# Reciprocals of the softmax denominators in the first attention: spread over partitions by products with the identity, or by GpSimd's transfers through DRAM

## The reference

```python
sc = jnp.einsum('...qd,...kd->...qk', qb, kk) * SCALE + bias      # causal mask inside
m = jnp.max(sc, axis=-1, keepdims=True)
p = jnp.exp(sc - m)
den = jnp.sum(p, axis=-1, keepdims=True)
o = jnp.einsum('...qk,...kd->...qd', p, vv) / den
# the three branches of B are added, each times its gate per row and head
```

## Time and profile before

| | |
|---|---|
| median of 3 runs | 2310.55 us (2309.71 to 2312.58) |
| profiled execution | 2309.23 us, span 2307.4 us |
| TensorE matmul busy | 2054.1 us, 89% |
| weight loads busy | 1079.7 us, 47% |
| VectorE busy | 999.7 us, 43% |
| ScalarE busy | 616.5 us, 27% |
| GpSimd busy | 184.1 us, 8% |
| mean granted TensorE clock | 0.954 of 2.4 GHz |

### The profile page before, as it was taken

How to read it: one execution, slowest core, us unless ns; L and a number is a source line. 1 busy time by engine, 2 the same in 40 slices (tenths; PEclk the granted TensorE clock), 3 DMA queues, 4 the chain that set the end, 5 groups by cost and what they waited for, 6 DMA issues and landing times.

```text
span 2307.4 us, 26770 instructions
## 1 busy us (share of the span) xinstructions
PE 2054.1 (89%) x10158; PEld 1079.7 (47%) x10158; DVE 999.7 (43%) x1830; ACT 616.5 (27%) x1191; POOL 184.1 (8%) x222
## 2 busy tenths in 40 slices
PE   7999999999999998989978986999749588959994
PEld 4555764444444444565566443333244466433331
DVE  2003652577872013687354244223156655252223
ACT  2003551000000013322254033334241344123332
POOL 3000110111110000121000001000010000000001
PEclk9999999999999999999999997999979899979997
DMA  8333002577664203112010026777442000066884
GB/s 277 99 86 123 30 2 73 203 244 264 237 237 146 82 16 119 37 37 73 1 56 1 19 115 219 297 300 278 163 166 73 1 1 1 1 230 261 325 323 185
DMA packets 103868, 311.64 MB, mean 135 GB/s; under 512 B 8839, under 2 KB 42791, under 8 KB 85312
## 3 DMA queue, kind: packets, MB, share of 16 engines
q1 hardware_dynamic: 73360, 178.50, 22.1%
q0 software_dynamic: 22576, 103.09, 12.7%
q10 hardware_dynamic: 7808, 28.35, 3.1%
HBM read 280.47 MB, written 34.68 MB: 137 GB/s over the span
## 4 chain that ended last, share of the span: by engine, by line
PE 76%; DVE 9%; issue 7%; PEld 2%; DMA 2%; ACT 1%; DVEq 0%; PEldq 0%; POOL 0%; POOLq 0%; ACTq 0%; SPq 0%
PE ps L2554 13%; PE ps L2293 10%; PE ps L302 8%; PE ps L327 7%; PE ps L1577 6%; PE ps L729 5%; PE ps L2275 5%; PE ps L764 4%; PE ps L1434 3%; PE ps L747 2%; DVE T L857 2%; PE ps L1553 2%; PE ps L2261 2%; PEld ps L1285 1%; PE ps L1285 1%
## 5 line engine op out<-in xcount | busy, mean ns | idle before, releaser
L2554 PE MATMUL ps<-wide 128*128 128x512 f32 x704 | 306.0, 594 | 2.3 <-issue 1.3
L2293 PE MATMUL ps<-wide,Z 128*64 x576 | 259.7, 604 | 4.0 <-DVE Z L2387 4.0
L2294 PE MATMUL ps<-T,Z 128*64 128x512 f32 x576 | 259.7, 605 | 0.0
L2554 PEld LDWEIGHTS ps<-wide 128*128 128x128 f32 x704 | 132.4, 190 | 171.8 <-issue 170.6
L793 ACT ACTIVATE T<-T,nm 128x128 f32<-128x128 f32 (+5 forms) x208 | 139.8, 672 | 171.7 <-DVE nm L857 171.7
L747 PE MATMUL ps<-ident,T 128*128 128x128 f32 x752 | 115.1, 284 | 46.6 <-DVE T L365 27.7
L2293 PEld LDWEIGHTS ps<-wide,Z 128*64 128x64 f32 x576 | 77.1, 139 | 158.0 <-issue 158.0
L1577 PE MATMUL ps<-wide 128*128 128x512 f32 (+1 forms) x384 | 149.7, 547 | 0.6 <-issue 0.6
L2275 PE MATMUL ps<-wide,Z 128*64 x288 | 134.6, 611 | 4.4 <-ACT Z L2348 4.4
L2276 PE MATMUL ps<-Z 128*64 128x512 f32 x288 | 134.7, 611 | 0.0
L1056 DVE SCALAR_TENSOR_TENSOR Z<-Z,wide 128x2048 f32<-128x2048 f32 x56 | 131.6, 2350 | 2.8
(11 more groups left out here) (350 smaller groups left out, 2807.7 us busy)
## 6 DMA issues: line engine op xcount, KB each, us to landing
wide<-in_experts SPq DMA_DIRECT2D x96, 1024.0 KB, 7.5
Z<-in_mod_w POOLq DMA_DIRECT2D x32, 1024.0 KB, 5.3
moe_out<-Z ACTq DMA_DIRECT2D x36, 512.0 KB, 5.0
X<-in_mod_w POOLq DMA_DIRECT2D x16, 1024.0 KB, 5.2
wide<-in_w_gate SPq DMA_DIRECT2D x22, 512.0 KB, 5.0
wide<-in_w_up SPq DMA_DIRECT2D x22, 512.0 KB, 6.8
wide<-in_w_in SPq DMA_DIRECT2D x10, 1024.0 KB, 10.9
wide<-in_w_down SPq DMA_DIRECT2D x10, 1024.0 KB, 5.1
```

The lines of the kernel that those rows point to most:

```text
L2293: pe.matmul(ps[low, p, :], mo.xT[:, p, c, low], w.columns(e, j, at), start=(c == 0), stop=(c == DK - 1))
L2294: last = pe.matmul(ps[high, p, :], mo.xT[:, p, c, high], mo.wgu[:, p, j, at:at + 512], start=(c == 0), stop=(c == DK - 1))
L2554: last = pe.matmul(self.gu.bank(u)[:, 0:self.n], w, self.rhs(c), start=(c == 0), stop=(c == DK - 1))
```

## The change

The first attention gets an argument `far`: a DRAM scratch of 16 x 8 x 128 floats and four buffers of 128 x 512 in the part of `X` that holds nothing at that time. With it

- TensorE leaves out L774 and the wait for `recips_done`, and the ring of PSUM banks has no entry for it.
- GpSimd, for each pack, waits for `recips_done`, stores `rd` (128 partitions x 8 floats) to DRAM with queries along the row, which makes 1,024 pieces of one float; waits until that has landed; and loads it back with two transfers, one for each head, each row of 128 floats four times into 64 partitions (64 x 4 pieces of 512 B). Between the store and the loads it waits for the pack four before to be scaled, whose buffer it takes.
- VectorE multiplies at step j+5 in place of j+3, after a wait for both loads, with both operands in SBUF.
- GpSimd issues the bias loads for group q+2 behind the spread of the last pack of group q, and adds a pack of B two packs later (the last two at the end).

The other two attentions of the kernel keep the old form; for them `far` is None. (Their `gpsimd` loop now returns at once; it had nothing to do there.)

```diff
--- before.py
+++ after.py
@@ -626,9 +626,14 @@
 
 
 
-    def __init__(self, k, packs, width, off_p, off_t, sbufs, tbanks, loads=None, side=None):
+    def __init__(self, k, packs, width, off_p, off_t, sbufs, tbanks, loads=None, side=None, far=None):
         super().__init__(k)
         self.packs, self.loads, self.sbufs, self.side = packs, loads or [], sbufs, side
+
+        self.far = far
+        self.behind = 5 if far else 3
+        if far:
+            self.rd_stored, self.rd_spread = k.recips_stored.reserve(16 * len(packs)), k.recips_spread.reserve(32 * len(packs))
         self.Pb = k.T[:, off_p:off_p + 4 * width].rearrange("p (b h n) -> p b h n", b=2, h=2)
         self.PT = k.T[:, off_t:off_t + 4 * width].rearrange("p (b h n) -> p b h n", b=2, h=2)
         self.units = [(pi, ui, u) for pi, pk in enumerate(packs) for ui, u in enumerate(pk["units"])]
@@ -647,7 +652,7 @@
                         owners.append("act" if turn % 2 else "dve")
                         turn += 1
             j = i - 2
-            if 0 <= j < len(self.units) and self.ends[self.units[j][0]] == j:
+            if not far and 0 <= j < len(self.units) and self.ends[self.units[j][0]] == j:
                 self.rb[self.units[j][0]] = len(owners)
                 owners.append("dve")
         self.wide = width > 512
@@ -764,7 +769,7 @@
                             last = pe.matmul(k.ps[64 * h:64 * h + 64, 7, ui * P:(ui + 1) * P], v(h),
                                              self.PT[:, j % 2, h, b * P:(b + 1) * P], start=(b == 0), stop=(b == nb - 1))
                 last.then_inc(k.out_full.sem, 1)
-                if self.ended(j) is not None:
+                if self.ended(j) is not None and not self.far:
                     pe.wait_ge(k.recips_done.sem, self.rd + pi + 1)
                     r = self.rb[pi]
                     self.t.may_fill(pe, r)
@@ -827,7 +832,7 @@
         if self.packs[0]["units"][0]["bias"] is None:
             ch.step(dve.memset(k.zeros, 0.0))
             ch.wait()
-        for i in range(N + 4):
+        for i in range(N + self.behind + 1):
             if i < N:
                 pi, ui, u = self.units[i]
                 n = u["n"]
@@ -870,8 +875,13 @@
                     dve.drain().then_inc(k.bias_used.sem, 1)
             if self.side:
                 self.side.vector(dve, ch, i)
-            pi = self.ended(i - 3)
-            if pi is not None:
+            pi = self.ended(i - self.behind)
+            if pi is not None and self.far:
+                dve.wait_ge(k.recips_spread.sem, self.rd_spread + 32 * (pi + 1))
+                dve.wait_ge(k.out_taken.sem, self.o_out + pi + 1)
+                raw = self.raw(pi)
+                dve.tensor_tensor(raw, self.split(pi, self.far[1](pi)), raw, ALU.mult).then_inc(k.packs_scaled.sem, 1)
+            elif pi is not None:
                 pk = self.packs[pi]
                 r = self.rb[pi]
                 self.t.await_full(dve, r)
@@ -915,15 +925,33 @@
 
     def gpsimd(self, pool, ch):
         k = self.k
-        todo = list(self.extra.items())
-        for q in range(2, len(self.loads)):
-
-            while todo and self.packs[todo[0][0]]["load"] < q - 2:
-                self._sum(pool, *todo.pop(0))
-            pool.wait_ge(k.bias_used.sem, self.b_used + q - 1)
-            self._load(pool, q)
-        for pi, x in todo:
-            self._sum(pool, pi, x)
+        if not self.far:
+            return
+        last = {pk["load"]: pi for pi, pk in enumerate(self.packs)}
+        for pi, pk in enumerate(self.packs):
+            self._spread(pool, pi)
+            q = pk["load"]
+            if last[q] == pi and q + 2 < len(self.loads):
+                pool.wait_ge(k.bias_used.sem, self.b_used + q + 1)
+                self._load(pool, q + 2)
+            if pi - 2 in self.extra:
+                self._sum(pool, pi - 2, self.extra[pi - 2])
+        for pi in range(len(self.packs) - 2, len(self.packs)):
+            if pi in self.extra:
+                self._sum(pool, pi, self.extra[pi])
+
+    def _spread(self, pool, pi):
+        k = self.k
+        rows, buf = self.far[0], self.far[1](pi)
+        pool.wait_ge(k.recips_done.sem, self.rd + pi + 1)
+        pool.dma_start(rows[pi].rearrange("c q -> q c"), k.rd[:, pi % 2, 0:8],
+                       allow_slow_non_contiguous=True).then_inc(k.recips_stored.sem, 16)
+        if pi >= 4:
+            pool.wait_ge(k.packs_scaled.sem, self.mul + pi - 3)
+        pool.wait_ge(k.recips_stored.sem, self.rd_stored + 16 * (pi + 1))
+        for h in range(2):
+            src = bass.AP(tensor=rows.tensor, offset=rows.offset + (8 * pi + h) * P, ap=[[0, 64], [2 * P, 4], [1, P]])
+            pool.dma_start(buf[64 * h:64 * h + 64, :].rearrange("p (a n) -> p a n", a=4), src).then_inc(k.recips_spread.sem, 16)
 
     def _sum(self, pool, pi, x):
         k = self.k
@@ -2749,6 +2777,7 @@
         k.token_landed = [tally(f"token_rows_landed_{i}") for i in range(NT)]
         k.y_stored = [tally(f"y_stored_{p}") for p in range(2)]
         k.out_stored = tally("out_stored")
+        k.recips_stored, k.recips_spread = tally("recips_stored"), tally("recips_spread")
         k.half_done, k.both_done = tally("half_done"), tally("both_done")
         k.mods_ready = sem("mods_ready")
         k.mod_landed = [tally(f"mod_weights_landed_{i}") for i in range(3)]
@@ -2853,7 +2882,8 @@
             packs.append(dict(base, units=slc, first=False, gate=gates[1]))
             packs.append(dict(base, units=win, first=False, gate=gates[2]))
             loads.append([bias_of(A_HEADS + rr), bias_of(A_HEADS + 4 + rr)])
-        projection.early = PairAttention(k, packs, 512, 7168, 9216, 1, 4, loads)
+        projection.early = PairAttention(k, packs, 512, 7168, 9216, 1, 4, loads,
+                                         far=(scratch["recips"], lambda pi: k.X[:, ST + pi % 4 // 2, 512 * (pi % 2):512 * (pi % 2) + 512]))
         add(projection.early)
 
         def mixT_units(w, starts, tiles):
@@ -3066,6 +3096,7 @@
                "h": [nc.dram_tensor(f"moe_rows_{l}", (n * P, D), F32, kind="Internal").ap() for l, n in enumerate((NT, ST))],
                "y": [nc.dram_tensor(f"moe_out_{l}", (pairs_bound(n * P), P, D), F32, kind="Internal").ap()
                      for l, n in enumerate((NT, ST))],
+               "recips": nc.dram_tensor("recip_rows", (16, 8, P), F32, kind="Internal").ap(),
                "away": nc.dram_tensor("rows_away", (NT * P, D), F32, kind="Internal").ap(),
                "mods": nc.dram_tensor("mod_rows", (2, 2, 6144), F32, kind="Internal").ap()}
     stages = two_blocks(nc, A, C, out, scratch)
```

## The result

The changed kernel takes 2426.16 us (median of 4 executions, 2424.93 to 2430.02) against 2311.46 for the kernel before beside it: ratio 1.05, 95% interval 1.0482 to 1.0518. That is 115 us slower, far above the range of the forecast.

What follows compares the result with a forecast made beforehand. TensorE was taken to bound the stage. Terms: -14.7 products, +1.6 VectorE, +6.5 cmp packs, +0.7 bias loads, +3.8 tail, +1.7 and +1.0 clock: +0.6 us, 2311.2 us. Own range 2306 to 2316; over all rivals 2301 to 2336.

Steps and rivals of the forecast that it cites:

- s: Time from issue to landing of GpSimd's DRAM store of the reciprocals: taken as 3.1 us, bounds 2.1 and 5.0.
- Rival B: Scattered store lands slowly while GpSimd stands still: +26 us, 2336, at s = 5.0; no bound beyond; chance 0.29.
- products gone, with VectorE's term: First attention: 14.7 us saved on TensorE, less 1.6 us for VectorE's moved multiplication.
- clock at the stage's start: TensorE's slower clock from gaps at one-unit (cmp) packs: +1.0 us, range 0 to 6.
- cmp and bias waits: VectorE waiting for the spread at one-unit packs, +6.5 us; bias loads issued behind the spread, +0.7 us (0 to 4).
- rival A: Quick round trip, s 2.1 and spread 2.4: no cmp or bias waits, tail +2.5, total -9.6 us, 2301; chance 0.25.
- each us of s: Cost of a slower store landing, at cmp waits, tail and bias loads together: some 10 us for each us.
- The removal: Products with the identity on TensorE's path: 0.98 us for each of 15 packs, 14.7 us saved, taken whole.
- The cmp packs: One-unit packs, whose store queues behind the previous spread: VectorE waits 1.9 us at three, 0.8 at the last, +6.5.
- The spreading loads: GpSimd's two loads back from DRAM: 2.7 us from first issue to second landing, range 2.4 to 3.3.
- The tail: Last reciprocals to next stage's start: 10.0 us in place of 6.2, +3.8, plus 1.7 for TensorE's clock.
- The list at the prediction's end: Signs to check: products gone, s under 2.6 or over 3.5, where VectorE waits for DMA, a 10 us tail.

Runs made afterwards that it cites:

- experiment 1: Changed kernel with each partition's eight reciprocals side by side in DRAM, 128 pieces of 32 B in place of 1,024 of 4 B: 2316.86 us, ratio 1.0022.
- experiment 13: Changed kernel, reciprocals turned by TensorE and stored as eight rows, multiplication at step j+6; cmp packs and the last pack keep the products: 2308.63 us, ratio 0.9986.
- experiment 2: Changed kernel storing 1,024 single floats 64 bytes apart in a DRAM scratch of its own, loads reading a constant: 2333.22 us.
- 7: As experiment 2, but with 16 bytes of DRAM from piece to piece: 2333.63 us.
- 11: Changed kernel storing the same 4 KB side by side in 512 pieces of 8 bytes, in the scratch and with the loads of experiment 2: 2334.45 us.
- experiment 5: Changed kernel without products and without transfers per pack; four spreads made once from a constant: 2301.22 us against 2310.56 before, ratio 0.9961.
- 14: As experiment 13, but with the products kept in the last three packs: 2308.75 us against 2312.95 before, ratio 0.9988.

## Why the prediction was wrong

**The step that failed: s.** The prediction took 3.1 us from bounds of 2.1 and 5.0, and it is 9.4. Both bounds came from rows that write long pieces; no row had pieces that share a word of DRAM. The lower bound also took 1.2 us of data out of a comparison that doesn't give them: a store of 512 KB lands in 2.9 us and a load of 256 KB in 3.0. That experiment 1 measured 1.7, which is 2.9 - 1.2, is luck. The long list of the weight load had priced the issue right (0.91 measured, 0.96 in the earlier trace rows), and I let that stand for what 1,024 pieces cost. The issue is a cost of GpSimd's and is 0.91 us whether the landing takes 2.6 (SBUF), 3.2 or 9.4; nothing about the landing is in the issue's length. The sentences that set the Trainium skill against this change pointed the right way. Of the Trainium skill's rule, in "DMA: Bandwidth & Descriptors" under "Specifications", that below 512 B a transfer becomes a read-modify-write, the runs here bear out the direction for 4-byte pieces, but no step at 512 B: eight rows of 512 B land in 1.6 us (experiment 13), 128 pieces of 32 B in 1.7, pieces of 4 B in 3.2 when 64 bytes apart and in 9.4 side by side. Whether anything is read and written back no trace shows.

**Rival B had the right mechanism.** It named GpSimd, standing still until each store has landed, and said that past 5 us every pack of 16 pays. The wait table has them: 16 waits of GpSimd, 14 of VectorE on L883. Its price below 5 us, some 10 us for each us of s, is what experiments 1 and 2 show: 1.5 us more of s, 15.0 us more of stage (162.5 against 147.5). From experiment 1 to the changed kernel it is 109 us for 7.7 us of s, 14 each, since the four-unit packs have joined. But it set the chance of B at 0.29 and closed the range where its own row ended, although it said itself that no row gave a bound beyond.

**Even with its s the forecast was too low.** The kernels with s from 3.2 to 3.7 (experiments 2, 7 and 11) took 2333 to 2334, about 22 us over the kernel before, not 0.6. The terms, each by the kernel that isolates it:

| term | predicted | measured | where |
|---|---|---|---|
| products gone, with VectorE's term | -13.1 | -10.7 | reciprocals, first to last, experiment 5 |
| clock at the stage's start | within +1.0 | none shown; 9.4 to 12.1 us by chance | first reciprocals of all kernels |
| tail without transfers | 0 | +1.1 | experiment 5 |
| cmp and bias waits, at s = 3.2 | +6.5 and +0.7 | +25.4, slower clock included | experiment 2 less 5, first to last reciprocals |
| cmp waits, at s = 1.7 | 0 (rival A) | +8.5 | experiment 1 less 5, first to last reciprocals |
| tail, at s = 1.7 | +2.5 (rival A) | +5.9 | experiment 1 less 5, 13.2 against 7.4; 3.3 of it after GpSimd's last sum |
| each us of s | about 10 | 10, then 14 | experiments 1 and 2, then after |

**The removal.** 0.98 us a pack were nearly right as a length: from the second A pack's reciprocals to the third's it is 8.98 us where it was 9.85, and to the fourth's 10.34 where it was 11.22. Of the 14.7 us 4.0 didn't come back, where the prediction had 1.6 for VectorE. TensorE's new wait, from the wait table of experiment 5, 199 to 333 us:

```profile
PE ps L769 <- DVE T L365: 3.4, 4, 0.9
```

Four times, once a round, TensorE now waits for a copy that VectorE makes late; before, its products never waited for one at that line. The prediction had named the place (0.4 us a round), but not this reason: each of the four copies stands right behind a gate multiplication that took 1.23 us beside GpSimd's sum (experiment 5). Three of the waits lie in the loop, 2.5 us, and leave 1.5 of the 4.0, about what the prediction had; the fourth, 0.9, is most of what the tail gained.

**The cmp packs** were taken too lightly, and this is the second step that failed. At s = 3.2, the forecast's own, the loop is 25.4 us longer than in experiment 5, where the prediction had 7.2 for them and the bias loads and 1.0 for the clock; VectorE waits 5.0 and 4.4 us at the first two cmp packs (experiment 2), where the prediction had 1.9. Rival A had them wait for nothing at s = 2.1. Experiment 1 has 1.7 and waits five times, 15.6 us in all, ahead of L883: once at each cmp pack, 10.0 together, and 5.5 in the tail. Its GpSimd timeline around the first cmp pack:

```profile
242.60 1.10 POOL L924 DMA_DIRECT2D Z<-bias_spread  x2
243.70 0.55 POOL L947 DMA_DIRECT2D recip_rows<-rd  x1
247.64 1.25 POOL L954 DMA_DIRECT2D X<-recip_rows  x2 [3.40 <-DVE wide L883]
```

Here the store takes 3.9 us to GpSimd's next instruction, where it took 2.0 to 2.2 at most other packs. It stands on the same queue behind the loads that were issued just before it, two of 128 KB and two bias tables of 256 KB, and the queue's packets last to 246.5. (The profile names L883 as what ended the wait; the one that L954 needs, of the pack four before, was over at 218.8.) The prediction had put the bias loads into GpSimd's time of issue, 1.1 us, and not into the queue. In experiment 1 that doubles s just where VectorE has no slack, and in experiment 2 the stores of the first two cmp packs land after 4.2 and 4.5 us in place of 3.2.

**The spreading loads** took more than the 2.7 us of the pair: 3.6 in the median from the first issue to the second landing in experiments 1 and 2 (2.9 for one, and the second issued 0.6 behind), and 3.7 for one alone in the changed kernel.

**The tail** is 18.6 us in the changed kernel (predicted 10.0), 12.3 at s = 3.2, so 2.3 over the prediction's own sum even there: 0.9 from the loads, and 1.4 from GpSimd's end (2.5 us to the next product in place of 1.1).

**The clock.** In the changed kernel TensorE's granted clock is 0.74 over the stage, and its busy time 146.0 us where experiment 5 has 120.9 for the same products. Those 25 us aren't simply added to the 115: in the chain from 290 to 315 us no product stands, so a slower one there costs nothing. At s = 3.2 (clock 0.88, busy 130.5) they do tell in part, between the waits; the prediction had +1.0 for this.

**Ledger of the changed kernel**, by the stage of each profiled execution: -8.0 for the products (133.5 in experiment 5 against 141.5; by the medians of the whole kernel -9), +14.0 for transfers and waits with a quick store (147.5 in experiment 1), +109.1 for the slow landing (256.6). Sum +115.1. The first step has 1.6 us of chance from the stage's start in it and would be -9.6 without.

**What would have shown it.** The list at the prediction's end worked as tests: s over 3.5 is B, and VectorE waiting at four-unit packs makes the forecast wrong. Both are read at once.

## What to carry to other kernels

A transfer's cost has three parts that rows must show each by itself: its issue, its place in the queue behind what was issued before, and its landing; a row with long pieces gives no bound for the landing of short ones, so a range must then stay open above. Where the result of a transfer goes back into the loop that issues it, count the whole turn (here 15.6 us) against the time of one pass (9.9) and ask at which latency the slack ends. If single values must go through DRAM, turn them into rows first (here one product and one copy, 0.27 us each): the store then costs 2.1 us in place of 10; but measure what leaving out the work is worth at all before paying for its replacement, since here experiment 5 gained 9 us. And when an engine's work is moved, look at what it will now run beside.

## What the runs showed of the hardware

- A store of 4 KB to DRAM in pieces of 4 bytes: 1.7 us when those of a partition lie side by side in order and can join, 3.2, 3.7 and 3.9 with 64, 16 and 8 bytes from piece to piece, and 9.4 when the pieces fill every word (7.6 when neighbours come from one partition; 4.9 for that order at 8 bytes, where the other has 3.9). 512 pieces of 8 bytes side by side: 3.7. Eight rows of 512 bytes: 1.6. The slow one has sent all its packets 2.2 us after the issue and is confirmed 7 us later.
- Loads that read rows just written in 4-byte pieces are slower: 3.7 us against 3.0 for the same load from a constant (2.9 for rows just written in 32-byte pieces, experiment 1), and 6.3 where all read the same two rows.
- VectorE's multiplications with both operands in SBUF take longer beside GpSimd's sum (1.26 us): 1.23 us in place of 0.17 for 128 x 8, and 1.10 in place of 0.69 for 128 x 512 (experiment 5, seven times).
- The issue of 1,024 pieces takes GpSimd 0.91 us, of 512 0.76, of the joined ones 0.54.
- From GpSimd's last sum to the next stage's first product are 1.1 us before, 1.8 in experiment 5, 2.5 in most, and 3.6 to 5.0 in experiments 1, 13 and 14. Transfers just ahead of it aren't the reason; it stays open.
